# Decoder-trunk step on one core: exponentials grouped ahead of copies, one-matmul tile sums, and the paged softmax placed inside the first attention

## The reference, cut to what matters

```python
h = x @ w_in                     # columns: qa ka va fa | ub vb | qc kc vc | pd
logf = log_sigmoid(fa + b_forget)
# A, prompt: 4 heads x 64, causal
f = cumsum(logf); p = softmax(q @ k.T / 8 + f_q - f_k); o_a = p @ v
# A, each sample row: 2048 paged rows and itself
k_all = concat(cache_k[page_table], ka); v_all = concat(cache_v[page_table], va)
o_a = softmax(q @ k_all.T / 8 + f_q - f_all) @ v_all
# B: chunked gating; C: dilated window attention; D: causal pooling
y = (sigmoid(x @ w_gate + b_gate) * branches @ w_branch).sum() @ w_out
x = LN(ALPHA * x + y); x = LN(ALPHA * x + moe(x))      # 16 experts, top 2
```

## Time and profile before

| | |
|---|---|
| median of 3 runs | 1567.37 us (1563.78 to 1569.9) |
| the profiled execution: time / span | 1567.51 us / 1565.7 us |
| mean granted TensorE clock | 0.949 |
| PE busy | 1419.9 us (91%) |
| DVE / ACT / POOL busy | 743.7 / 432.2 / 309.0 us |
| bias, attention A, stage 4, attention C, in us from the start | 193 to 213, 213 to 304, to 442, 471 to 556 |

### The profile page before, as it was taken

How to read it: one execution, slowest core, us unless ns; L and a number is a source line. 1 busy time by engine, 2 the same in 40 slices (tenths; PEclk the granted TensorE clock), 3 DMA queues, 4 the chain that set the end, 5 groups by cost and what they waited for, 6 DMA issues and landing times.

```text
span 1565.7 us, 20000 instructions
## 1 busy us (share of the span) xinstructions
PE 1419.9 (91%) x7544; PEld 1068.0 (68%) x7544; DVE 743.7 (47%) x1302; ACT 432.2 (28%) x721; POOL 309.0 (20%) x233
## 2 busy tenths in 40 slices
PE   7999978799998899999999999999938799999980
PEld 3466465444454599999999999878736466666650
DVE  1266445422124442243443444455666466777746
ACT  1111134201015411111111111212124455665536
POOL 1138920045174000000000000000231521221220
PEclk9969999999999999999999999999958899999995
DMA  7346630255331022232222332422376999888645
GB/s 219 104 134 222 207 127 1 71 172 186 132 99 42 35 77 72 77 104 77 73 93 77 106 142 77 145 78 81 120 300 256 312 302 305 289 300 272 202 164 221
DMA packets 75196, 237.70 MB, mean 152 GB/s; under 512 B 17029, under 2 KB 27476, under 8 KB 61422
## 3 DMA queue, kind: packets, MB, share of 16 engines
q1 hardware_dynamic: 48630, 160.73, 28.4%
q0 software_dynamic: 17792, 59.20, 12.8%
q10 hardware_dynamic: 8704, 16.84, 3.1%
HBM read 213.49 MB, written 65.74 MB: 178 GB/s over the span
## 4 chain that ended last, share of the span: by engine, by line
PE 75%; DMA 8%; DVE 6%; POOL 4%; ACT 3%; issue 3%; SPq 0%; POOLq 0%; DVEq 0%; ACTq 0%
PE ps L460 15%; PE ps L462 14%; PE ps L461 14%; PE ps L1224 11%; DMA tmp_yd<-b,b 7%; PE ps L1205 5%; PE ps L593 4%; POOL b L1967 3%; PE ps L1321 2%; PE ps L1358 2%; PE ps L1409 1%; ACT b L1590 1%; PE ps L522 1%; PE ps L1221 1%; PE ps L1239 1%
## 5 line engine op out<-in xcount | busy, mean ns | idle before, releaser
L460 PE MATMUL ps<-b,b 128*128 128x344 f32 (+1 forms) x1360 | 470.3, 346 | 9.3 <-DVE b L987 3.8
L461 PE MATMUL ps<-b,b 128*128 128x344 f32 (+1 forms) x1360 | 465.8, 342 | 0.0
L462 PE MATMUL ps<-b,b 128*128 128x344 f32 (+1 forms) x1360 | 465.8, 342 | 0.0
L460 PEld LDWEIGHTS ps<-b,b 128*128 128x128 f32 x1360 | 255.2, 188 | 30.8 <-issue 10.7
L462 PEld LDWEIGHTS ps<-b,b 128*128 128x128 f32 x1360 | 255.1, 188 | 19.4 <-issue 0.9
L461 PEld LDWEIGHTS ps<-b,b 128*128 128x128 f32 x1360 | 255.0, 188 | 17.0 <-issue 0.6
L1224 PE MATMUL ps<-b,b 128*128 128x512 f32 (+1 forms) x640 | 258.1, 561 | 0.0
L1224 PEld LDWEIGHTS ps<-b,b 128*128 128x128 f32 x640 | 122.3, 194 | 121.7 <-issue 117.1
L1056 POOL DMA_INDIRECT tmp_xs<-b,b x36 | 44.9, 1247 | 634.4 <-issue 574.9
L1205 PE MATMUL ps<-b,b 128*128 128x128 f32 (+1 forms) x782 | 122.8, 286 | 51.0 <-DMA b<-tmp_xs 18.6
L987 DVE TENSOR_TENSOR b<-b,b 128x2048 fp32r<-128x2048 f32 x64 | 146.3, 2289 | 45.3 <-ACT b L678 42.7
(11 more groups left out here) (265 smaller groups left out, 1261.9 us busy)
## 6 DMA issues: line engine op xcount, KB each, us to landing
b<-in_w SPq DMA_DIRECT2D x96, 1024.0 KB
b<-in_w_merge SPq DMA_DIRECT2D x32, 640.5 KB, 4.5
tmp_xs<-b ACTq DMA_DIRECT2D x32, 514.0 KB, 4.0
b<-tmp_xs SPq DMA_DIRECT2D x32, 514.0 KB
b<-in_w_in SPq DMA_DIRECT2D x8, 1024.0 KB, 8.6
b<-in_xT SPq DMA_DIRECT2D x4, 1024.0 KB, 12.4
b<-in_w_out SPq DMA_DIRECT2D x4, 1024.0 KB, 7.7
b<-in_x SPq DMA_DIRECT2D x8, 512.0 KB, 4.0
```

The costliest lines, as they stand in the source:

```text
L460: mm(out, hi, mhi, start=start, stop=False)
L461: mm(out, hi, mlo, start=False, stop=False)
L462: return mm(out, lo, mhi, start=False, stop=stop)
```

## The change

- The 16 value products move three slots forward, one in each of slots 0 to 15; the window softmax steps move to slots 11 to 13 (from 13 to 15). The exponential of the window part moves to tile 4 of `vpd` (from 6).
- The paged softmax moves into `attention(0)`: on DVE into `side_a` (units 0, 2, 3, 10) and `norm` (pairs 2, 3, 5), on PE into `side_a` of the value products, on ACT behind unit 9. Its small results lie in free columns of bank 7.
- The sums of all tiles ahead are made by one matmul for all heads and tiles; DVE adds them while it moves `fb` out. 28 matmuls go and one comes.
- ACT, in both attentions, takes both exponentials of an odd unit ahead of the even unit's copies, and copies bank 5 of the odd units in place of DVE.
- POOL's and SP's instructions are the same, in the same order.

```diff
-        SLOTS_A = {i: ["top", "spread", "total"][i:i + 1] if i < 3 else [i - 3] for i in range(18)}
+        SLOTS_A = {i: [i] if i < 16 else [] for i in range(18)}
         for i, step in enumerate(("top_c", "spread_c", "total_c")):
-            SLOTS_A[13 + i].append(step)
-        SLOTS_A[17].append(15)
+            SLOTS_A[11 + i].append(step)
...
 # PE, the bias
                     for q in range(4):
-                        t = half * 4 + q
-                        o_ = ps[:, 6 + n % 2, q * P:(q + 1) * P]
-                        mm(o_, lf[:, t, h:h + 1].to_broadcast([P, P]), tri_neg[:], start=True, stop=(t == 0))
-                        if t:
-                            m = mm(o_, lpre[:, t, h:h + 1].to_broadcast([P, P]), ones_neg[:], start=False, stop=True)
+                        m = mm(ps[:, 6 + n % 2, q * P:(q + 1) * P], lf[:, half * 4 + q, h:h + 1].to_broadcast([P, P]), tri_neg[:],
+                               start=True, stop=True)
                     m.then_inc(S("fb_mm"), 1)
                     n += 1
+                    if n == 2:
+                        mm(ps[:, 3, 0:32], ones_neg[:], lpre[:].rearrange("p t h -> p (t h)"), start=True, stop=True).then_inc(S("fb_mm"), 1)
...
 # PE, before and in attention(0)
+                pe.wait_ge(S("ltot"), 1)
+                mm(ps[:, 5, 0:32], trisA[:], ltot[:], start=True, stop=True).then_inc(S("lsuf"), 1)
...
+            def side_a(i):
+                if i == 2:
+                    pe.wait_ge(S("dmx"), 1)
+                    tr(ps[:, 7, W:W + P], mx[:]).then_inc(S("dmx_tr"), 1)
+                elif i == 3:
+                    pe.wait_ge(S("dmc"), 1)
+                    mm(ps[:, 7, W:W + 32], mcol[0:32, 0:1].to_broadcast([32, P]), ident[0:32, 0:32],
+                       start=True, stop=True).then_inc(S("dmb"), 1)
+                elif i == 5:
+                    pe.wait_ge(S("dsum"), 1)
+                    mm(ps[:, 7, W:W + 32], ones[:], dsum[:], start=True, stop=True).then_inc(S("dtot"), 1)
...
 # ACT, attention(br)
-                for u in range(16):
+                for u in range(0, 16, 2):
+                    weights(u + 1, 0)
+                    weights(u + 1, 1)
+                    blocks(u, 0)
+                    blocks(u, 1)
                     for hh in range(2):
-                        blocks(u, hh)
-                        if u < 15:
-                            weights(u + 1, hh)
+                        blocks(u + 1, hh)
+                        high_blocks(u + 1, hh)
+                    if br == 0 and u == 8:
+                        act.wait_ge(S("dsh"), 1)
+                        act.activation(sA[:], sA[:], ACT.Exp).then_inc(S("dex"), 1)
+                    if u < 14:
+                        weights(u + 2, 0)
+                        weights(u + 2, 1)
...
 # DVE, the bias (each of the 8 turns n), and attention(0)
-                dve.tensor_copy(fb[:, n // 2, (n % 2) * 512:(n % 2) * 512 + 512], ps[:, 6 + n % 2, :]).then_inc(S("fb"), 1)
+                dve.tensor_tensor(fb[:, n // 2, (n % 2) * 512:(n % 2) * 512 + 512].rearrange("p (t r) -> p t r", r=P),
+                                  ps[:, 6 + n % 2, :].rearrange("p (t r) -> p t r", r=P),
+                                  first.rearrange("p (t o) -> p t o", o=1).to_broadcast([P, 4, P]), ALU.add).then_inc(S("fb"), 1)
...
+            def softmax_step(i):
+                if i == 2:
+                    dve.wait_ge(S("dmx_tr"), 1)
+                    dve.tensor_reduce(mcol[0:32, :], ps[0:32, 7, W:W + P], AX.X, ALU.max).then_inc(S("dmc"), 1)
+                elif i == 3:
+                    dve.wait_ge(S("dmb"), 1)
+                    link(dve.tensor_copy(mrow[:], ps[:, 7, W:W + 32]))
+                    dve.tensor_tensor(sA[:], sA[:], mA, ALU.subtract).then_inc(S("dsh"), 1)
+                elif i == 5:
+                    dve.wait_ge(S("dtot"), 1)
+                    link(dve.reciprocal(drec[:], ps[:, 7, W:W + 32]))
+                    dve.tensor_tensor(sA[:], sA[:], rA, ALU.mult).then_inc(S("dp"), 1)
...
-            decode_softmax(0, sA, lambda: qk_evict("qkc", 1, 1), lambda: None)
+            qk_evict("qkc", 1, 1)
             qk_evict("qkc", 2, 2)
             key_sums_c(0)
             key_sums_c(1)
```

More of the change, by code:

```diff
@@ L1382, in tail_a @@
                 project("qkc", 0)
-            attention(0, bias_a, lambda k, h: va[:, k, h * 64:h * 64 + 64], lambda i: None, tail_a)
+            def side_a(i):
[9 more added lines that the diff above has]
+                    mm(ps[:, 7, W:W + 32], ones[:], dsum[:], start=True, stop=True).then_inc(S("dtot"), 1)
+            attention(0, bias_a, lambda k, h: va[:, k, h * 64:h * 64 + 64], side_a, tail_a)
             def top(br):
@@ L1430, in heads_out @@
                 m.then_inc(S("heads"), 1)
-            steps = {"top": lambda: top(0), "spread": lambda: spread(0), "total": lambda: total(0),
-                     "top_c": lambda: top(1), "spread_c": lambda: spread(1), "total_c": lambda: total(1)}
+            steps = {"top_c": lambda: top(1), "spread_c": lambda: spread(1), "total_c": lambda: total(1)}
             def decode_slot(i):
@@ L1767, in _ @@
                 key_sums(6 + i)
+            dve.wait_ge(S("fb_mm"), 3)
+            link(dve.tensor_copy(dsum[:], ps[:, 3, 0:32]))
             for n in range(8):
-                dve.wait_ge(S("fb_mm"), n + 1)
-                dve.tensor_copy(fb[:, n // 2, (n % 2) * 512:(n % 2) * 512 + 512], ps[:, 6 + n % 2, :]).then_inc(S("fb"), 1)
+                if n >= 2:
+                    dve.wait_ge(S("fb_mm"), n + 2)
+                first = dsum[:].rearrange("p (t h) -> p h t", h=H)[:, n // 2, 4 * (n % 2):4 * (n % 2) + 4]
+                dve.tensor_tensor(fb[:, n // 2, (n % 2) * 512:(n % 2) * 512 + 512].rearrange("p (t r) -> p t r", r=P),
+                                  ps[:, 6 + n % 2, :].rearrange("p (t r) -> p t r", r=P),
+                                  first.rearrange("p (t o) -> p t o", o=1).to_broadcast([P, 4, P]), ALU.add).then_inc(S("fb"), 1)
             def decode_out(br, bank):
@@ L1821, in norm @@
                     dve.wait_ge(S("pv"), 8 * br + i + 1)
-                    if br:
+                    if br == 0:
+                        softmax_step(i)
+                    else:
                         for n, b in enumerate(VALUES_C.get(i, ())):
@@ L1843, in attention @@
                         norm(u // 2 - 1)
-                    blocks(u, 0)
-                    blocks(u, 1)
+                    if u % 2 == 0:
+                        blocks(u, 0)
+                        blocks(u, 1)
                     side(u)
@@ new lines, in side_a @@
+            def side_a(u):
+                if u == 0:
+                    dve.wait_ge(S("lgb"), 16)
+                    dve.wait_ge(S("lsuf"), 1)
+                    link(dve.tensor_tensor(ltot[:], ps[:, 5, 0:32], lgb[:], ALU.add))
+                    link(dve.tensor_tensor(lfs[:, 0], lfs[:, 0],
+                                           ltot[:].rearrange("p (b o h) -> p b o h", b=NB, o=1).to_broadcast([P, NB, 16, H]), ALU.add))
+                elif u == 1:
+                    key_sums(15)
+                elif u == 2:
+                    dve.wait_ge(S("ks"), 16)
+                    link(dve.scalar_tensor_tensor(s16, s16, SCALE, lfs[:, 0], ALU.mult, ALU.add))
+                elif u == 3:
+                    dve.wait_ge(S("selfd0"), N("selfd0", 16))
+                    link(dve.tensor_scalar(sA[:, :, 16, :], sA[:, :, 16, :], SCALE, None, ALU.mult))
+                    dve.tensor_reduce(mx[:, 0:32].rearrange("p (b h) -> p b h", b=NB), sA[:].rearrange("p b r h -> p b h r"),
+                                      AX.X, ALU.max).then_inc(S("dmx"), 1)
+                elif u == 10:
+                    dve.wait_ge(S("dex"), 1)
+                    dve.tensor_reduce(dsum[:].rearrange("p (b h) -> p b h", b=NB), sA[:].rearrange("p b r h -> p b h r"),
+                                      AX.X, ALU.add).then_inc(S("dsum"), 1)
@@ L1859, in _ @@
             dve.sem_inc(S("wpb0"), 1)
-            dve.wait_ge(S("lgb"), 16)
-            dve.wait_ge(S("lsuf"), 1)
-            link(dve.tensor_tensor(ltot[:], ps[:, 6, 0:32], lgb[:], ALU.add))
-            dve.sem_inc(S("ba"), 1)
-            link(dve.tensor_tensor(lfs[:, 0], lfs[:, 0],
-                                   ltot[:].rearrange("p (b o h) -> p b o h", b=NB, o=1).to_broadcast([P, NB, 16, H]), ALU.add))
-            dve.wait_ge(S("ks"), 16)
-            dve.wait_ge(S("selfd0"), N("selfd0", 16))
-            s16 = sA[:, :, 0:16, :]
-            link(dve.scalar_tensor_tensor(s16, s16, SCALE, lfs[:, 0], ALU.mult, ALU.add))
-            link(dve.tensor_scalar(sA[:, :, 16, :], sA[:, :, 16, :], SCALE, None, ALU.mult))
             def decode_softmax(br, s, before_total, between):
```

27 lines of the change are left out of this document (13 added, 14 removed).

## The result

The changed kernel takes 1658.29 us (median of 4 runs, 1657.07 to 1662.08), the kernel before 1566.51 beside it. The ratio is 1.060 with a 95% interval of 1.057 to 1.063: 92 us slower. The forecast was 1656 with a range of 1636 to 1675. The profiled execution took 1657.07 us with a span of 1655.2, against 1567.5 and 1565.7 before.

What follows compares the result with a forecast made beforehand. PE, busy 91% of the span, was taken as the bound. Stage 4 +98.2, bias -4.3, attention A -2 and C -3.5 sum to +88.4; on 1567.5 that gives 1656 us, range 1636 to 1675.

Steps and rivals of the forecast that it cites:

- The place and the number of the waits: Stage 4: PE waits before value products 2, 3, 5, 6, 7 and 8, not 4 or 9 to 15.
- The lead survives: Rival, stage 4: value loads not held back by PE's turn, so the change gives its gains alone; 1551.5 us, 3%.
- Only slot 2 pays: Rival, stage 4: keys far enough ahead after slot 2, so 17.0 + 1.75 stands against the gains; 1570 us, 2%.
- The clock does not come back: Rival, stage 4: projections after waits run wholly at 1.2 GHz, losing 5.3 more six times; 1688 us, 5%.
- The length of the loop: Stage 4: transposes, key sum, key loads, multiply, value load and landing take 15.2 us, 15.5 for odd slots; five waits, 76.9.
- a query row that lands 3.8 after its own start: Loop link on POOL: three key loads, 1.67 us of issue, then a query row landing 3.8 later; together 5.5 us.
- the rival of a shorter loop: Stage 4: query row lands in 2.3 us instead of 3.8, values in 5.4 instead of 5.7; 1647 us, 8%.
- The clock: Stage 4: PE restarts at 1.2 instead of 2.4 GHz after each of six waits, losing 1.75 us each, 10.5 us.
- Stage 4 in sum: Stage 4: 17.0 for slot 2, 76.9 for five waits, 10.5 for the clock, -8.6 and +2.4; +98.2 us.
- the last two terms: Stage 4: removed softmax wait, slow projection and small matmul, -8.6 us; products 14 and 15 ahead of the last projection, +2.4.
- The bias: Before attention A: the new forget bias brings the first scores earlier, -4.3 us, or -1 if the clock stays low.
- The attentions: Attentions A and C: ACT's new order gains some 3.5 us each, paged softmax costs 1.5 in A; -2 and -3.5.

Runs made afterwards that it cites:

- The three kernels with a lag: The changed kernel with each value product one, two or three slots later: 1583.26, 1562.85 and 1566.16 us.
- the one with POOL's order turned: The changed kernel, with POOL loading values 2 and 3 before the first keys and keys c after values c+2: 1571.62 us, ratio 1.006 to the kernel before.
- the kernel with three slots: The changed kernel with value product s in slot s+3, all else kept: 1566.16 us, ratio 1.001 to the kernel before.
- the three profiles with three slots and POOL's order as it was: The changed kernel with products three slots later, and two builds on it with ACT's old order in units 0 to 7 or everywhere: 1566.16, 1559.09, 1569.47 us.
- The kernel with ScalarE's order alone: The kernel before with only ACT's new order of copies and exponentials and its bank 5 copies: 1568.32 us, ratio 1.003.
- the old order in the light units: The changed kernel with products three slots later and ACT's order of before in units 0 to 7 of each attention: 1559.09 us.

## Why the prediction was right

The time was forecast as 1567.5 + 88.4 and the span grew by 89.5. The mechanism of the loss is the one that was forecast. That the total came within some 1 us is luck: the terms are off by more, and cancel.

**The place and the number of the waits: right.** Slots 2, 3, 5, 6, 7 and 8, and not 4 nor 9 to 15. The three kernels with a lag and the one with POOL's order turned show the cause from both sides: give the loads a lead, or take them from behind the keys, and the waits of 14 us go. "The lead survives" and "Only slot 2 pays" fell. So did "The clock does not come back".

**The length of the loop: 1.3 us too long on average.** Forecast 15.2, and 15.5 for odd slots, measured 13.75 in slot 3: 2.2 from the transposes to POOL's wake (forecast 2.0), 3.7 from the first key load to the multiply (5.5), 1.8 for the multiply, 0.2 to the issue, 5.9 to the landing (6.0 for an odd slot). The step that was mis-sized is "a query row that lands 3.8 after its own start". The row that POOL loads at 347.13 belongs to the next multiply; the one for this multiply came a turn earlier. The multiply at 349.15 waits for the last of the three keys. From issue to landing, all keys from 340 to 470 took this (first line), the query rows that (second):

```profile
DMA to landing us min/median/max: 2.3/2.4/4.4
DMA to landing us min/median/max: 3.1/3.5/3.8
```

So the rival of a shorter loop had the right sign and the wrong cause: the keys at 2.4 decide, not the query row; the value loads had a median of 5.7 as forecast. The five waits are 70.4 us instead of 76.9, and slot 2 is 18.1 instead of 17.0. The estimate of 4.4 us for the gather, worked out from the fit in the Trainium skill, DMA: Bandwidth & Descriptors, section Anatomy of one DMA, is not what the landings here show (5.4 to 7.1). The estimate of 2.3 by the same fit for 128 KB agrees with the least and the median of the key loads (2.3 and 2.4), and not with the query rows of the same size (3.1 to 3.8).

**The clock: 10.5 forecast, 12.9 found.** Windows over two restarts, after the waits of slots 2 and 3:

```profile
330.00:336.00 6.00, 3.85 (x19) 1.64 (x20) 0.00 (x0) 0.00 (x0) 0.00 (x0) 0.50 0.22 91
336.00:338.00 2.00, 2.00 (x5) 0.77 (x4) 0.00 (x0) 0.00 (x0) 0.00 (x0) 0.62 0.00 0
357.00:361.00 4.00, 3.96 (x20) 1.80 (x21) 0.00 (x0) 0.37 (x1) 2.83 (x2) 0.50 0.08 25
361.00:363.00 2.00, 2.00 (x5) 0.83 (x5) 0.00 (x0) 0.00 (x0) 0.00 (x0) 0.90 0.62 147
```

The six products took 6.4 us more than at full clock (three by 0.87, three by 1.26), the five projections behind the first five waits 4.9 more than 7.13 each, the transposes behind the last 0.5, and the tile of the sample rows behind them 1.1 (2.99, where the kernel with three slots has 1.93).

**Stage 4 in sum: +98.2 forecast, +94.6 measured.** 88.5 + 12.9 - 8.6 + 2.4 is 95.2, within 0.6 us of it, so the last two terms fit as forecast, together. Nothing tried them one by one. With the ring open at most 3.8 of the 8.6 us were gained: the three profiles with three slots and POOL's order as it was have 133.9 to 137.9 for the stage, the kernel before 137.7.

**The bias: right at its place**, -4.3 us at the first scores. Its items (0.3, 1.3, 3.5, 3.6 and a last add of 0.7) add up to 9.4 and not to the 9.1 that was used, a slip of 0.3. That a gain there is a gain of the kernel is not shown (the bias alone: ratio 1.001).

**The attentions: wrong, and of the wrong sign in A.** The step that failed is "What goes is an exponential between two copies ... Over the wide units I get some 3.5 us for each attention". It looked at the wide units only and took the light ones to be neutral. In those ACT has little else, so that an exponential put ahead of the copies is itself what PE waits for, and behind the 1.55 us wait stand 8 us and more of half clock. Forecast -2, measured +5.1: 4.7 for the light units, 2.7 for the paged softmax (forecast 1.5), -2.3 for the wide ones. The bounds given, up to +4, did not hold A in this execution; in the five with the same A it is +2.6 to +5.1. In C it is -0.9 instead of -3.5, but five kernels with C as in the kernel after lie between 81.8 and 87.4 and two with C as before at 83.8 and 87.0, so the profiles do not tell what the order is worth there. The kernel with ScalarE's order alone, slower by 5 us over ten runs, says that in both together it is a loss.

**The range.** About half of all the bounds together was given as 1644 to 1668. By the bounds as listed the lower end is 1648 (half of 3.9 + 1 + 2.1 + 8.2). The range that was stated is wider, and the time lies in either.

**What made the total fit.** Stage 4 was forecast 3.6 us too dear and A and C together 9.7 too cheap. The expert stage, 6.0 shorter in this execution, covered most of the rest. That is the luck, since no part of the change explains it: other kernels with the same code there had 318.6 to 328.4.

## What to carry to other kernels

A stage in which the bound engine never waits says nothing about what it costs to reorder: before moving a consumer forward, write down what its supplier's load stands behind in its queue, and whether one of those things needs the consumer's own turn. If so, the price per turn is the full length of that ring. Either cure opens it: the consumer moved back (94 of the 94.6 us here, with three slots) or the loads moved forward (85). When such waits are gone, compare the two engines' pace per turn (here 9.4 against 8.5 us), and look for the consumer's shortest turn, before counting on what a removed stall gives; and when an engine's work is put ahead of its copies, look at the lightest unit first.

## What the hardware did that was not expected

- A pause of 1.55 us between short matmuls (0.3 to 0.7 us groups) was followed by a granted clock of 0.50 for at least 8 us, with PE busy for 3.55 to 4.00 of each 4 us. With the old order in the light units the clock stayed at 1.00 over the same stretch, and with the change's order the slow stretch was shorter in another execution (0.83 instead of 0.53 over 10 us).
- The same 1 MB gather took 5.4 to 7.1 us to land in the kernel after, and 9.6 once in the kernel with three slots.
- A key load of 128 KB landed in 2.4 us (median of 18; 15 of them have no gather right ahead of them on POOL's queue), where the earlier trace rows has a median of 4.2 with a gather ahead of most of them.
